# Output weights' low parts on VectorE, and two splits moved within the steps of the last two attentions

## The reference, cut to what matters

```python
def even_mixer(h, w_in, sinks, rel_bias_table, w_out):
    ...
    o_a = stick_breaking_attention(hd(q_a, SB_HEADS), hd(k_a, SB_HEADS), hd(v_a, SB_HEADS))
    o_b = sliding_window_attention(hd(q_b, SW_HEADS), hd(k_b, SW_KV_HEADS), hd(v_b, SW_KV_HEADS),
                                   sinks, rel_bias_table)
    return jnp.concatenate([o_a, o_b], axis=-1) @ w_out

def mla_mixer(h, positions, w_down, q_norm, w_uq, kv_norm, w_ukv, w_o):
    ...
    return mla_attention(q_nope, q_rope, k_nope, k_rope, v) @ w_o
```

## Time and profile before

| what | value |
|---|---|
| time, median of 3 runs | 1458.34 us (1457.06 to 1458.89) |
| the profiled execution | 1458.99 us |
| its span, first to last instruction | 1457.2 us |
| PE busy | 1364.8 us (94%) |
| DVE busy | 855.6 us (59%) |
| ACT busy | 634.9 us (44%) |
| POOL busy | 282.5 us (19%) |
| mean granted TensorE clock | 0.961 of full |

### The profile page before, as it was taken

How to read it: one execution, slowest core, us unless ns; L and a number is a source line. 1 busy time by engine, 2 the same in 40 slices (tenths; PEclk the granted TensorE clock), 3 DMA queues, 4 the chain that set the end, 5 groups by cost and what they waited for, 6 DMA issues and landing times.

```text
span 1457.2 us, 28178 instructions
## 1 busy us (share of the span) xinstructions
PE 1364.8 (94%) x10956; PEld 1209.3 (83%) x10956; DVE 855.6 (59%) x1696; ACT 634.9 (44%) x1246; POOL 282.5 (19%) x354
## 2 busy tenths in 40 slices
PE   7899999899899988999998998899999789999998
PEld 6898888789788887999888855899988656799986
DVE  5566666645568876788645345544446555544444
ACT  4344444433144435666445425543334246543343
POOL 0002322211344321132201102111200122111200
PEclk9999999999799999999998969999999989999999
DMA  7312111024321134455555401455454331255552
GB/s 291 116 60 82 67 59 60 31 88 149 117 83 59 59 131 159 175 187 186 181 194 174 162 1 58 145 181 194 173 202 145 115 116 59 87 176 193 180 189 100
DMA packets 26503, 188.87 MB, mean 130 GB/s; under 512 B 2944, under 2 KB 3072, under 8 KB 4128
## 3 DMA queue, kind: packets, MB, share of 16 engines
q1 hardware_dynamic: 25632, 182.51, 35.1%
q0 software_dynamic: 768, 4.92, 1.0%
HBM read 186.37 MB, written 1.05 MB: 129 GB/s over the span
## 4 chain that ended last, share of the span: by engine, by line
PE 85%; DVE 7%; ACT 4%; issue 1%; DVEq 1%; DMA 1%; POOLq 0%; POOL 0%; ACTq 0%; SPq 0%
PE ps L561 48%; PE ps L509 13%; PE ps L809 5%; PE ps L1188 2%; PE ps L660 1%; PE ps L649 1%; PE ps L1050 1%; PE ps L541 1%; PE ps L534 1%; PE ps L774 1%; PE ps L828 1%; PE ps L533 1%; PE ps L908 1%; PE ps L478 1%; DVE mx L1726 1%
## 5 line engine op out<-in xcount | busy, mean ns | idle before, releaser
L561 PE MATMUL ps<-h_hi,w_hi 128*128 128x256 f32 x1208 | 345.5, 286 | 5.0 <-DVE h_lo L1785 5.0
L561 PE MATMUL ps<-h_lo,w_hi 128*128 128x256 f32 x1208 | 344.7, 285 | 0.0
L561 PE MATMUL ps<-h_hi,w_lo 128*128 128x256 f32 x1208 | 344.5, 285 | 0.0
L1815 DVE TENSOR_TENSOR w_lo<-ring,w_hi 128x1024 fp32r<-128x1024 f32 x111 | 139.2, 1254 | 270.5 <-ACT w_hi L1315 270.4
L1315 ACT ACTIVATE w_hi<-ring 128x1024 fp32r<-128x1024 f32 x119 | 126.2, 1060 | 321.5 <-PE ps L561 321.1
L561 PEld LDWEIGHTS ps<-h_hi,w_hi 128*128 128x128 f32 x1208 | 234.8, 194 | 6.6 <-issue 6.6
L561 PEld LDWEIGHTS ps<-h_lo,w_hi 128*128 128x128 f32 x1208 | 234.8, 194 | 0.0
L561 PEld LDWEIGHTS ps<-h_hi,w_lo 128*128 128x128 f32 x1208 | 234.8, 194 | 0.0
L509 PE MATMUL ps<-oT_r,ring_r 128*128 128x256 f32 x512 | 147.3, 288 | 0.0
L1821 DVE TENSOR_TENSOR w_lo<-ring,w_hi 128x1024 fp32r<-128x1024 f32 x111 | 139.7, 1258 | 0.0
L1317 ACT ACTIVATE w_hi<-ring 128x1024 fp32r<-128x1024 f32 x119 | 124.5, 1046 | 0.0
(11 more groups left out here) (406 smaller groups left out, 2786.4 us busy)
## 6 DMA issues: line engine op xcount, KB each, us to landing
ring<-in_weights SPq DMA_DIRECT2D x170, 1024.0 KB, 4.8
arena<-in_aux POOLq DMA_DIRECT2D x1, 2112.0 KB, 12.7
grow<-in_rows POOLq DMA_DIRECT2D x3, 512.0 KB, 3.9
cst<-in_consts SPq DMA_DIRECT2D x1, 1497.5 KB, 14.4
x<-in_x SPq DMA_DIRECT2D x1, 1024.0 KB, 5.0
arena<-in_swbias POOLq DMA_DIRECT2D x1, 1024.0 KB, 7.7
out<-xn SPq DMA_DIRECT2D x4, 256.0 KB, 2.2
sml<-in_small SPq DMA_DIRECT2D x1, 536.0 KB, 5.6
```

The costliest lines, as they stand in the source:

```text
L561: m = pe.matmul(dst, l[a], r[b], start=first and n == 0 and a == b, stop=last and n == len(pairs) - 1 and a == 1)
L1815: dve.tensor_tensor(w_lo[:, half_of(u0, m), WH:], ring[:, (u0 + m) % RING, WH:], w_hi[:, half_of(u0, m), WH:].bitcast(F32), ALU.subtract). ...
```

## The change

GpSimd no longer touches the output weights: its eight subtractions in each of the two attentions go to VectorE, at the end of steps 1 and 2 (units 0 and 1, two halves each) and 11, 12, 15 and 16 (one half each). On ScalarE `out_weights` now stands at the end of a step. Units 0 and 1 are still split in steps 0 and 1, but behind that step's sigmoids or exponentials. Units 2 and 3 are split in halves: the first in steps 10 and 14, with the wait for `unit_done`, the second in steps 11 and 15.

```diff
--- ScalarE (block.scalar)
-            def split_unit(u0, m, i=0):
-
+            def high_p(u0, m, i=0):
                 arrived(act, u0 + m, i)
                 act.activation(w_hi[:, half_of(u0, m), WH:], ring[:, (u0 + m) % RING, WH:],
                                ACT.Copy).then_inc(w_hi_p, 1)
+            def high_d(u0, m, i=0):
                 act.activation(w_hi[:, half_of(u0, m), 0:WH], ring[:, (u0 + m) % RING, 0:WH],
                                ACT.Copy).then_inc(w_hi_d, 1)
+            def split_unit(u0, m, i=0):
+                high_p(u0, m, i)
+                high_d(u0, m, i)
...
-            def out_weights(u0, s):
-                if s in (0, 1):
-                    split_unit(u0, s)
-                if s in (9, 13):
-                    m = (s - 1) // 4
-                    act.wait_ge(unit_done, u0 + m - 1)
-                    split_unit(u0, m)
+            def out_weights(u0, s, s0=0):
+                if s in (s0, s0 + 1):
+                    act.wait_ge(unit_done, u0)
+                    split_unit(u0, s - s0)
+                if s in (10, 14):
+                    act.wait_ge(unit_done, u0 + s // 4 - 1)
+                    high_p(u0, s // 4)
+                if s in (11, 15):
+                    high_d(u0, s // 4)
...
             for s in range(H + 3):
-                out_weights(U["even_out"], s)
                 if s < SB_HEADS:
                     act.wait_ge(a_scores, s + 1)
...
                 if s >= 3 and s % 2 == 0:
                     out_high((s - 4) // 2)
+                out_weights(U["even_out"], s)
...
             for s in range(H + 3):
-                out_weights(U["mla_out"], s)
                 if s < H:
                     softmax_exp(SW_HEADS + s, s % 3)
...
                     out_high(KT + (s - 4) // 2)
+                out_weights(U["mla_out"], s)
--- VectorE (block.vector)
+            def out_weights(u0, name, s, s0=0):
+                if s in (s0 + 1, s0 + 2):
+                    split_unit(u0, name, s - s0 - 1)
+                if s in (11, 15):
+                    first_half(u0, name, s // 4)
+                if s in (12, 16):
+                    second_half(u0, name, s // 4 - 1)
...
                     out_low((s - 4) // 2)
+                out_weights(U["even_out"], "even_out", s)
...
                     out_low(KT + (s - 4) // 2)
+                out_weights(U["mla_out"], "mla_out", s)
--- GpSimd (block.gpsimd)
-            def split_whole(u0, name, m):
-                pool.wait_ge(w_hi_p, SPLIT[name] + m + 1)
-                pool.sem_inc(apart, 1)
-                pool.tensor_tensor(w_lo[:, half_of(u0, m), WH:], ring[:, (u0 + m) % RING, WH:],
-                                   w_hi[:, half_of(u0, m), WH:].bitcast(F32), ALU.subtract).then_inc(w_lo_p, 1)
-                pool.wait_ge(w_hi_d, SPLIT[name] + m + 1)
-                pool.sem_inc(apart, 1)
-                pool.tensor_tensor(w_lo[:, half_of(u0, m), 0:WH], ring[:, (u0 + m) % RING, 0:WH],
-                                   w_hi[:, half_of(u0, m), 0:WH].bitcast(F32), ALU.subtract).then_inc(w_lo_d, 1)
...
-            for m in range(4):
-                split_whole(U["even_out"], "even_out", m)
...
-            for m in range(4):
-                split_whole(U["mla_out"], "mla_out", m)
```

## The result

The changed kernel takes 1443.99 us (median of 13 runs, 1439.81 to 1450.04), the kernel before, run beside it, 1457.41 us (13 runs, 1452.68 to 1462.53). The ratio is 0.9914, 95% interval 0.9896 to 0.9932.

The account below looks back on a forecast made before the run. TensorE, busy 94% of the span, was taken to set the time; -3.4 - 4.1 + 1.0 - 2.6 = -9.1 us took the profiled 1458.99 to 1449.9, and the median, 0.65 lower, to 1449.2 us; 8-in-10 range 1445 to 1453.5.

Parts of the forecast that it names:

- The even start, -3.4: Even attention's start: without GpSimd's halves, TensorE's wait before head 0's transposes goes, -3.4 us.
- The softmax heads, -4.1: Even attention, steps 10, 14, 15, 16: waits of 4.2 us go, less 0.1 us allowed for step 12, -4.1 us.
- just borne: Even attention, step 11: a maximum starting 2.27 us after the scores left TensorE's transposes no listed idle time.
- The tight place: Even attention, step 12: VectorE's second half delays the next maximum to 2.2 us after the scores; 0.1 us allowed.
- MLA's start, +1.0: MLA's first steps: table load behind the first maximum and both splits in the chain delay head 1's transposes, +1.0 us.
- MLA's waits, -2.6: MLA, steps 10 and 14: two TensorE waits of 1.31 us each go, -2.6 us.
- VectorE as bound: Rival, softmax steps: halves of steps 11, 12, 15, 16 lose 2 to 5 us of the gain, 1451.5 to 1454.5; 15%.
- waits replaced: Rival: ScalarE's halves push the next exponentials as whole splits did; only even start less MLA's 1.0 remains, 1456 us; 6%.
- the halves on the path: Rival: every VectorE half delays an awaited maximum, 20 us in against 10.2 us of waits removed, 1468 us; 3%.
- the clock at the stage changes: Rival, all stages: half clock 7 us longer or shorter, 3.5 us either way, 1446 or 1452.5; within the forecast's case.
- the early clock: Rival, even start: full clock from about 842 instead of 867, about 11 us more gain, 1438 us; 4%.
- The rule weighed there: Even start: by the skill's rule a gap-free start would soon get 2.4 GHz; judged not borne out for small products.

Follow-up runs that it names:

- act_alone_b: The changed kernel with the low parts back on GpSimd, so only ScalarE's new order remains, in both attentions: 1456.31 us, ratio 0.999.
- before_look: The kernel before, unchanged, one more profile: 1457.33 us.
- after_look: The changed kernel, unchanged, one more profile: 1451.03 us.
- after_gap: The changed kernel plus five unused VectorE subtractions in step 0 of the even attention, putting TensorE's wait back: 1448.13 us, ratio 0.9933.
- even_only: The changed kernel with MLA put back to that of the kernel before, so only the even attention is changed: 1451.07 us, ratio 0.9945.
- dve_alone: The changed kernel with ScalarE's splits in their old order, low parts still on VectorE, in both attentions: 1451.25 us, ratio 0.9948.
- after: The first profile of the changed kernel, no further edit: the profiled execution took 1442.09 us.
- after_again: The changed kernel, unchanged, run once more: 1442.53 us, ratio 0.9894; its profiled execution took 1451.11 us.
- both_warm_b: The changed kernel with MLA's earlier table load and later splits, 17 unread 512-column products in the even start and 14 in MLA's: 1441.44 us, ratio 0.9886.
- after_fill_b: The changed kernel with one unread 512-column product in each of steps 3, 4 and 5 of the even attention: 1445.36 us, ratio 0.991.
- before_fill_b: The kernel before with one unread 512-column product in each of steps 3, 4 and 5 of the even attention: 1459.69 us, ratio 1.0015.
- mla_both_b: The changed kernel with MLA's exponential table loaded earlier and its units 0 and 1 split in steps 2 and 3: 1438.82 us, ratio 0.9867.

## Why the prediction was too small

- **The even start, -3.4.** Right: 36.63 to 33.08 us is -3.55, by the cause that was named (1.01 and 0.63 us in place of 4.64 and 2.54; act_alone_b turns it round). Nothing took the wait's place.
- **The softmax heads, -4.1.** The term was too small: -5.07. A wait costs more than its listed idle time. A step without any takes 3.57 us; step 10 took 5.53 before, 1.96 us more for a wait of 1.77, and step 14 took 5.09, 1.52 more for 1.31. Steps 11 and 12, with no wait listed, took 3.66 and 3.72, so the 2.27 us that the prediction called just borne already cost 0.15. The tight place was named rightly and allowed 0.1 us; it costs 0.23, in step 14. The four waits of these steps and the one of the start are five, not the four that the prediction counts.
- **MLA's start, +1.0.** Right, slightly low: +1.1 against before_look, +1.5 against the first profile. The second transposes come 11.29 us after the first scores in place of 10.19, with the table load behind the first maximum.
- **MLA's waits, -2.6.** -3.0, again for the 0.2 us on top of each.
- **The sum of these** is -3.6 - 5.1 + 1.1 - 3.0 = -10.6 us from before_look to after_look, in place of -9.1. The rivals of VectorE as bound, of waits replaced and of the halves on the path all fell: of steps 10 to 14 four take 3.57 us and one 3.80.
- **Outside the steps.** The prediction put nothing there in its sum, and 3.5 us either way as the rival of the clock at the stage changes. The two profiles differ by +1.5 us between the norm and MLA's start and by -0.8 behind MLA's norm, which makes -9.9. The other 3.6 us between them lie ahead of the even attention, where the code is the same.
- **The clock is the step that failed.** The prediction had the half clock of the even start last until the output pieces, and gave the early clock 4%, outside the range, on the strength of 20.00 us busy of 20.00 at 0.50. In 12 or 13 of 20 executions of the changed kernel it happened, by times and mean clocks; the one profile among them shows it. Its price was wrong too. By its own terms, half of 25 us less 3, it would be 9.5 us and not 11; it is 33.08 - 26.98 = 6.1, since the clock comes back at 849.5, not at 842. The median is an execution of that group; the other, with the forecast's clock, lies at 1448.6 to 1451.1, beside the predicted 1449.2. One stretch of 20 us from one execution showed that the clock can stay down; I read it as showing that it must.
- **The chances.** Those of the cases add up to 0.92 for faster and 0.03 for slower; 0.91 and 0.04 were written.
- **The rule weighed there.** The Trainium skill, "TensorE: Matmul & The Clock Gate", Part 1, says that "activity releases the throttle". I wrote that the trace does not bear it out. The runs say less than either: a gap-free start was at 0.50 for 17.1 us in one profile and for 30.7 in another, and one with a gap of 4.38 us for 17.1 us too.

**What stays open.** What decides in one execution of the changed kernel between an end at 19.5 and at 33.0 us after the first scores, and how often the kernel before has an earlier end than 36.6, which its mean clocks point to and no profile shows. So how much of the changed kernel's faster group it owes to the change, and not to the draw, is not shown either: the landmarks show 10.6 us in the steps at the late clock, and 6.1 us more where the clock comes back early. It is not the wait (after_gap), and not MLA's part (even_only). GpSimd's part is not settled: dve_alone, without it, ends at 32.9 in its profile, but half of its executions have mean clocks of 0.967; act_alone_b, with it, ends at 29.9. That wide products hold the clock up is what three of four profiles with 17 or 42 of them show; the fourth shows that they don't make it certain.

## What to carry to other kernels

Work on GpSimd that "nobody waits for" can hold up TensorE when VectorE runs beside it: look at what the same VectorE instruction takes with and without it. Where a wait can be seen, count some 0.2 us more than its idle time; and compare the steps' lengths, since a step can be late with no wait listed. Where a stretch runs at half clock, take more than one profile before a sum rests on where it ends, and give its other end a chance of its own.

## What the runs showed of the hardware

- With GpSimd's subtraction of 128 x 1024 running, two cumulative products of 128 x 128 took 5.25 us in place of 1.01 and two products 2.79 in place of 0.63, and an operation on 128 x 2 numbers 2.43 in place of 0.23; before GpSimd's first start they were undisturbed (act_alone_b).
- In the even attention's start, TensorE's granted clock fell from 1.00 to 0.50 some 2.2 to 2.6 us after the first small products (64 rows, 128 and 256 columns) in every kernel without a filler, though TensorE was busy, and came back 17.1 to 34.1 us after that; in equal code after 17.1 us (after) and after 30.7 (after_again, after_look). With 17 or 42 products of 512 columns more it stayed at 1.00 in three profiles of four and was at 0.50 for 10.2 us in the fourth (both_warm_b); with three more it was at 0.50 for 23.9 and 27.3 us (after_fill_b, before_fill_b).
- ScalarE's table load for the exponentials takes 1.28 us and stands behind the wait of the first exponential (1175.76, after); behind an exponential of one column, put earlier, it lay in idle time 8 us ahead of MLA's first scores (mla_both_b).
